# Three of eight k pairs by seven block products in each gate/up slice of a hybrid encoder block

## The chip, the cores and the metric

The kernel runs on one core of one Trainium2 chip. Its time is the device time of one execution in microseconds; the median of 3 runs of the kernel before is 1122.85 us (1122.55 to 1123.35).

## What is computed

One layer of an encoder block on 256 tokens of width 2048, in float32: RMSNorm, a projection, four mLSTM heads and four differential attention heads, an output projection, and then the part that matters here, SwiGLU with a hidden width of 5632:

```python
def swiglu(h, w_gate, w_up, w_down):
    return (jax.nn.silu(h @ w_gate) * (h @ w_up)) @ w_down

x = x + mixer(rms_norm(x, norm1_w), ...)
x = x + swiglu(rms_norm(x, norm2_w), w_gate, w_up, w_down)
```

## The kernel before

Every product with a weight matrix is made of three matmuls. An operand `a` is split in `a_hi` (a rounded to TensorE's fp32r) and `a_lo = a - a_hi`, and TensorE adds up `hi x w_lo + lo x w_hi + hi x w_hi`. The activations stand turned (`act_hi`, `act_lo`: 16 k tiles of 128 rows by 256 tokens); the weights are streamed.

The weights come in chunks of 128 x 1024 floats (512 KB). SyncE loads each into one of four places of `w_raw`; ScalarE writes `w_hi` from it, VectorE `w_lo`, both into one of four places (`SPLIT`), and TensorE uses them. Four semaphores carry this: `raw_landed`, `hi_done`, `lo_done` and `chunk_used`. ScalarE may write place n % 4 once chunk n - 4 is used; SyncE may load a raw place once VectorE has split what was there. Each engine has its own queue, in the order in which the program is written, and one use of a split chunk is called a step.

The input projection (96 chunks), the output projection (32) and the first of the eleven gate/up slices are written out. A slice is 512 columns of gate and the same 512 of up, for both token tiles, over 16 k tiles. Slices 2 to 11 run in a loop (`Fori`) on TensorE, ScalarE, VectorE and SyncE. The down projection follows (2 x 44 chunks).

In the looped slices two of the eight pairs of k tiles are handled by seven block products in place of eight. The two token tiles by the two k tiles of a pair are a 2 x 2 matrix of blocks, and the two k tiles by the gate's and the up's 512 columns are another. Seven products of sums of blocks suffice (`q1`, `q5`, `q7`, `q6` in the four `aux` banks, the other three right into `acc`), each of three matmuls: 21 in place of 24. The sums of activation blocks (E7, E5, E6, E3) are made once, in the first slice (`sum_hi`, `sum_lo`); those of weight blocks by VectorE in each slice, in place in `w_raw` (`weight_sums`: one of 1024 columns and two of 512 for a pair). A pair is four steps, of 3, 6, 6 and 6 matmuls; a single step has 12. So a slice has 12 single steps and 2 x 4, 20 steps and 186 matmuls.

Three steps behind the second pair ScalarE copies `q1` and VectorE combines the `aux` banks and adds them to the gate banks (`scaled`, with `pre_ready`) and, at the next slice's start, to the up banks (`hidden`). ScalarE then takes the SiLU of the gate (`gate`, `gate_act`), VectorE the product (`hid_ready`), TensorE turns it (`turn_hidden`), and both split it into `hid_hi` and `hid_lo`. TensorE waits at a slice's start for `gate_act`, behind the second step for `hid_ready`, and before the first pair for `hid_lo_done`.

Of the kernel before, what the change touches and what calls it, by code (L numbers as in the profile page):

```python
# [33 lines left out]
P = 128  # L34
# [16 lines left out]
RAW = 4  # L51
# [22 lines left out]
STEPS = 2 * 6 + 2 * 4  # L74
STEP0 = FF0 + FF_CHUNKS - STEPS
DOWN_STEP0 = STEP0 + FF_SLICES * STEPS
# [6 lines left out]
RELEASE = (-3, -2, -1, 0, 1, 2, 3, 4, 5, 8, 9, 10, 11, 12, 15, 16)  # L83
# [3 lines left out]
def step_raw(c):  # L87
    return c if c < 5 else c - 2 if c < 12 else c - 4

# [21 lines left out]
def hybrid_block_kernel(nc, x, x_turned, params, gate_bias, gate_w, weights, out):  # L111
    ctx = ExitStack()
    with ctx:
# [108 lines left out]
        seven = sb("seven", [3, NG], F32, ff)  # L222
        sum_hi = hid_hi[:, KF - 4:KF, :].rearrange("p k s -> p (k s)")
        sum_lo = hid_lo[:, KF - 4:KF, :].rearrange("p k s -> p (k s)")
        ff.close()
# [14 lines left out]
        evac_step = sem("evac_step")  # L240
        first_landed = sem("first_landed")
# [105 lines left out]
        def _(sp):  # L347
# [6 lines left out]
            for n in range(1, 8):  # L354
                if n < 5:
                    sp.dma_start(xt[:, xt_parts[n], :], x_turned[:, xt_parts[n], :]).then_inc(xt_landed[n], 16)
                if n >= RAW:
                    c = slice(NG * (n - RAW), NG * (n - RAW + 1))
                    sp.dma_start(res[:, :, c], x_t[:, :, c]).then_inc(x_landed[n - RAW], 16)
                    sp.wait_ge(lo_done, n - (RAW - 1))  # L360
                load(slice(n, n + 1), n % RAW)
            with sp.Fori(2, (FF0 + FF_CHUNKS) // RAW) as i:
                for k in range(RAW):
                    sp.wait_ge(lo_done, i * RAW + (k - (RAW - 1)))
                    load(bass.ds(i * RAW + k, 1), k)
# [4 lines left out]
            with sp.Fori(0, 2 * KF // RAW) as i:  # L370
                for k in range(RAW):
                    sp.wait_ge(lo_done, i * RAW + (DOWN_STEP0 + k - (RAW - 1)))
                    load(bass.ds(i * RAW + (DOWN0 + k), 1), k)
# [8 lines left out]
        def _(pool):  # L382
# [22 lines left out]
            pool.dma_start(w_if[:], gate_w).then_inc(wif_landed, 16)  # L405
            pool.dma_start(bias_if[:], gate_bias).then_inc(bias_landed, 16)
# [10 lines left out]
        def _(pe):  # L417
# [243 lines left out]
            def summed(e, j):  # L661
                cols = slice(2 * P * e + P * j, 2 * P * e + P * (j + 1))
                return sum_hi[:, cols], sum_lo[:, cols]

            q1, q5, q7, q6 = aux[2], aux[3], aux[0], aux[1]

            def pair(n, j):
                c, k = PAIR_STEP[j], PAIR_K[j]
                begin, end = j == 0, j == 1
                pe.wait_ge(lo_done, n + (c + 1))  # L670
                three(q1, *tile(k, 0), c % SPLIT, 0, begin, end).then_inc(chunk_used, 1)
                pe.wait_ge(lo_done, n + (c + 2))
                three(acc[0], *tile(k + 1, 0), (c + 1) % SPLIT, 0, False, end)
                three(acc[2], *summed(E3, j), (c + 1) % SPLIT, 1, begin, False).then_inc(chunk_used, 1)
                pe.wait_ge(lo_done, n + (c + 3))
                three(q5, *summed(E5, j), (c + 2) % SPLIT, 0, begin, end)
                three(q7, *summed(E7, j), (c + 2) % SPLIT, 1, begin, end).then_inc(chunk_used, 1)
                pe.wait_ge(lo_done, n + (c + 4))
                three(acc[1], *tile(k + 1, 1), (c + 3) % SPLIT, 0, False, end)
                three(q6, *summed(E6, j), (c + 3) % SPLIT, 1, begin, end).then_inc(chunk_used, 1)  # L680

            def ff_slice(i):
                n = i * STEPS + STEP0
                for c in range(STEPS):
                    if c == 0:
                        pe.wait_ge(gate_act, i * 2)
                    if c == PAIR_STEP[0]:
                        pe.wait_ge(hid_lo_done, i * 2)
                        pair(n, 0)
                    if c == PAIR_STEP[1]:  # L690
                        pair(n, 1)
                    if c in GATE_STEPS or c in UP_STEPS:
                        q = GATE_STEPS.index(c) if c in GATE_STEPS else UP_STEPS.index(c)
                        banks = acc[0:2] if c in GATE_STEPS else acc[2:4]
                        pe.wait_ge(lo_done, n + (c + 1))
                        for kk in range(2):
                            for t in range(TT):
                                begin = q == 0 and kk == 0 and (c in GATE_STEPS or t == 1)
                                end = q == 5 and kk == 1 and c in UP_STEPS
                                mm = three(banks[t], *tile(2 * q + kk, t), c % SPLIT, kk, begin, end)  # L700
# [812 lines left out]
```

## Time and profile before

| | us |
|---|---|
| median of 3 runs | 1122.85 |
| the profiled execution | 1125.04 |
| its span, first to last instruction | 1123.2 |
| TensorE busy with matmuls | 1113.3 |
| TensorE busy loading weights | 922.0 |
| VectorE busy | 734.6 |
| ScalarE busy | 576.8 |
| DMA, mean rate | 189 GB/s |

The span is what the rows can be laid against. Matmuls are pipelined: each is shown for some 0.39 us, while the next starts some 0.23 us after it, so TensorE's pace is read from start to start. Where VectorE's or ScalarE's instructions stand in one row with a count, the time is that of the whole run of them.

### The profile page before, as it was taken

What the parts mean: (1) busy time and instruction counts of PE and PEld (TensorE: products, weight loads), DVE (VectorE), ACT (ScalarE), POOL (GpSimd) and SP (SyncE); (2) the same over time, 40 slices, a digit from 0 to 9 for tenths busy, and PEclk for the clock granted to TensorE, in tenths of its full rate; (3) what the DMA queues carried; (4) which work ended last, traced back from release to release, by engine and by line L of the source; (5) the groups of instructions that cost most, each with busy time, mean ns of one, the idle gap of its engine ahead of it and who ended that gap; (6) DMA issues with size and microseconds to landing.
All of it is one profiled execution on the core that took longest, in us unless ns stands there. A gap on an engine that the chain in (4) does not pass through costs nothing.

```text
span 1123.2 us, 14985 instructions
## 1 busy us (share of the span) xinstructions
PE 1113.3 (99%) x5020; PEld 922.0 (82%) x5020; DVE 734.6 (65%) x876; ACT 576.8 (51%) x718; POOL 4.5 (0%) x20
## 2 busy tenths in 40 slices
PE   8999999999999999999999999999999999999998
PEld 6888887888888888888888888888888888888886
DVE  5566546764565566788787788788788644454443
ACT  7566466754545455446455455555555443343341
POOL 1000000000000000000000000000000000000000
PEclk8999999999999999999999999999999999999999
DMA  9555544564465646466566565565565756656554
GB/s 345 184 165 191 172 147 132 185 205 154 146 197 172 202 164 211 150 201 211 181 205 205 187 205 201 175 221 179 181 220 168 223 189 195 195 190 197 194 188 131
DMA packets 59796, 212.46 MB, mean 189 GB/s; under 512 B 6752, under 2 KB 6752, under 8 KB 59760
## 3 DMA queue, kind: packets, MB, share of 16 engines
q1 hardware_dynamic: 59552, 211.84, 57.1%
q8 instruction: 26, 0.43, 0.2%
q10 hardware_dynamic: 144, 0.05, 0.0%
q14 instruction: 10, 0.08, 0.0%
q0 software_dynamic: 64, 0.07, 0.0%
HBM read 209.83 MB, written 2.10 MB: 189 GB/s over the span
## 4 chain that ended last, share of the span: by engine, by line
PE 98%; DMA 1%; DVE 1%; ACT 0%; SPq 0%; issue 0%; ACTq 0%
PE acc L431 15%; PE acc L434 15%; PE acc L433 15%; PE acc L655 11%; PE acc L653 11%; PE acc L654 11%; PE aux L434 4%; PE aux L433 4%; PE aux L431 4%; PE aux L445 2%; PE aux L654 2%; PE aux L653 2%; PE aux L655 2%; DMA w_raw<-in_weights 1%; PE aux L495 0%; DVE res L1450 0%
## 5 line engine op out<-in xcount | busy, mean ns | idle before, releaser
L1060 DVE TENSOR_TENSOR w_lo<-w_raw,w_hi 128x1024 fp32r<-128x1024 f32 x231 | 280.8, 1223 | 241.1 <-ACT w_hi L750 119.6
L1393 DVE TENSOR_TENSOR w_lo<-w_raw,w_hi 128x1024 fp32r<-128x1024 f32 (+1 forms) x200 | 227.4, 1167 | 50.6 <-ACT w_hi L1008 23.6
L653 PE MATMUL acc<-w_lo,act_hi 128*128 128x512 f32 x520 | 203.2, 391 | 0.0
L655 PE MATMUL acc<-w_hi,act_hi 128*128 128x512 f32 x520 | 202.5, 389 | 0.0
L654 PE MATMUL acc<-w_hi,act_lo 128*128 128x512 f32 x520 | 202.3, 389 | 0.0
L750 ACT ACTIVATE w_hi<-w_raw 128x1024 fp32r<-128x1024 f32 x143 | 149.2, 1056 | 82.0 <-PE acc L434 73.9
L431 PE MATMUL acc<-w_lo,act_hi 128*128 128x512 f32 x448 | 179.1, 400 | 3.3 <-DVE w_lo L1060 3.3
L434 PE MATMUL acc<-w_hi,act_hi 128*128 128x512 f32 x448 | 175.7, 392 | 0.0
L433 PE MATMUL acc<-w_hi,act_lo 128*128 128x512 f32 x448 | 175.6, 392 | 0.0
L1011 ACT ACTIVATE w_hi<-w_raw 128x1024 fp32r<-128x1024 f32 x120 | 125.5, 1056 | 55.6 <-PE acc L655 32.2
L1032 ACT ACTIVATE w_hi<-w_raw 128x1024 fp32r<-128x1024 f32 x80 | 84.9, 1061 | 132.2 <-PE aux L434 132.2
L655 PEld LDWEIGHTS acc<-w_hi,act_hi 128*128 128x128 f32 x520 | 97.6, 188 | 20.4
L653 PEld LDWEIGHTS acc<-w_lo,act_hi 128*128 128x128 f32 x520 | 97.6, 188 | 20.0
L654 PEld LDWEIGHTS acc<-w_hi,act_lo 128*128 128x128 f32 x520 | 97.7, 188 | 19.9
L431 PEld LDWEIGHTS acc<-w_lo,act_hi 128*128 128x128 f32 x448 | 84.8, 189 | 22.4 <-issue 4.7
L434 PEld LDWEIGHTS acc<-w_hi,act_hi 128*128 128x128 f32 x448 | 84.8, 189 | 18.0
L433 PEld LDWEIGHTS acc<-w_hi,act_lo 128*128 128x128 f32 x448 | 84.9, 190 | 16.9
L431 PE MATMUL acc<-w_lo,hid_hi 128*128 128x512 f32 x176 | 68.6, 390 | 0.0
L431 PE MATMUL aux<-w_lo,hid_hi 128*128 128x512 f32 x176 | 68.5, 389 | 0.0
L434 PE MATMUL aux<-w_hi,hid_hi 128*128 128x512 f32 x176 | 68.5, 389 | 0.0
L434 PE MATMUL acc<-w_hi,hid_hi 128*128 128x512 f32 x176 | 68.5, 389 | 0.0
L433 PE MATMUL aux<-w_hi,hid_lo 128*128 128x512 f32 x176 | 68.5, 389 | 0.0
(250 smaller groups left out, 1274.4 us busy)
## 6 DMA issues: line engine op xcount, KB each, us to landing
w_raw<-in_weights SPq DMA_DIRECT2D x391, 512.0 KB, 4.2
res<-in_x SPq DMA_DIRECT2D x4, 512.0 KB, 10.8
out<-res SPq DMA_DIRECT2D x8, 256.0 KB, 3.8
xt<-in_x_turned SPq DMA_DIRECT2D x3, 512.0 KB, 9.4
xt<-in_x_turned SPq DMA_DIRECT2D x2, 256.0 KB, 4.3
w_raw<-in_weights SPq DMA_DIRECT2D x2, 256.0 KB, 3.8
w_if<-in_gate_w POOLq DMA_DIRECT2D x1, 64.0 KB, 6.7
par<-in_params ACTq DMA_DIRECT2D x1, 47.0 KB, 3.6
```

The lines of the kernel that those rows point to most:

```text
L431: pe.matmul(bank[:], hi[:, k, tok], w_lo[:, slot, cols], start=first and kk == 0, stop=False)
L433: pe.matmul(bank[:], lo[:, k, tok], w_hi[:, slot, cols], start=False, stop=False)
L434: mm = pe.matmul(bank[:], hi[:, k, tok], w_hi[:, slot, cols], start=False, stop=last and kk == len(kts) - 1)
L445: mm = pe.transpose(banks[t][:, P * b:P * (b + 1)], src[:, t, P * b:P * (b + 1)], ident[:])
L653: pe.matmul(bank[:], hi, w_lo[:, slot, cols], start=start, stop=False)
L654: pe.matmul(bank[:], lo, w_hi[:, slot, cols], start=False, stop=False)
L655: return pe.matmul(bank[:], hi, w_hi[:, slot, cols], start=False, stop=stop)
L750: act.activation(w_hi[:, slot, :], w_raw[:, slot, :], ACT.Copy).then_inc(hi_done, 1)
L1011: act.activation(dst, w_raw[:, step_raw(c) % RAW, :], ACT.Copy).then_inc(hi_done, 1)
L1032: act.activation(w_hi[:, c, :], w_raw[:, c, :], ACT.Copy).then_inc(hi_done, 1)
L1060: dve.tensor_tensor(w_lo[:, slot, :], w_raw[:, slot, :], w_hi[:, slot, :].bitcast(F32), ALU.subtract).then_inc(lo_done, 1)
L1393: dve.tensor_tensor(w_lo[:, c % SPLIT, cols], w_raw[:, slot, cols], w_hi[:, c % SPLIT, cols].bitcast(F32), ALU.subtract).then_inc(lo_done, 1)
```

## The change

A third pair of k tiles goes by seven products (k tiles 10 and 11, beside 12, 13 and 14, 15), in slices 2 to 11. The order of steps in such a slice is now a string, `ggggPguPuPuuu` (g a gate step, u an up step, P a pair of four steps); before it was five gate steps, a pair, a gate step, two up steps, a pair, four up steps. A slice has 10 single steps and 3 x 4, 22 steps. `plan()` lists every step of the program, and all engines' loops are written out from that list. `w_raw` has eight places in place of four, and a load waits for the last use of what stands in its place (`LAST_USE`). The tile `seven` is gone; its contents stand in `stage` and `gated`. The third pair's activation sums (`third_hi`, `third_lo`) are made in the first slice. The evacuation begins two steps behind the last pair (`EVAC_AT` 20, `PAIR_END` 18), with four of VectorE's operations in front of the next split in place of three. TensorE waits at a slice's start for `pre_ready` in place of `gate_act`. The loads of `gate_w` and `gate_bias` go from GpSimd's queue to ScalarE's, behind its work for chunk 1. The code also holds a way to handle pairs of the down projection, which `DOWN_PAIRS = ((), ())` leaves unused.

```diff
-RAW = 4
+RAW = 8
-GATE_STEPS = (0, 1, 2, 3, 4, 9)
-UP_STEPS = (10, 11, 16, 17, 18, 19)
-PAIR_STEP = (5, 12)
-PAIR_RAW = (5, 10)
-PAIR_K = (12, 14)
+SLICE_ORDER = "ggggPguPuPuuu"
+HALF = SLICE_ORDER.count("g")
+N_PAIRS = SLICE_ORDER.count("P")
+PAIR_K = [12, 14, 10][:N_PAIRS]
+EVAC_AT = 20
...
 SyncE
-            with sp.Fori(1, FF_SLICES) as i:
-                for j in range(FF_CHUNKS):
-                    sp.wait_ge(lo_done, i * STEPS + (STEP0 + RELEASE[j]))
-                    load(bass.ds(i * FF_CHUNKS + (FF0 + j), 1), j % RAW)
+            for n in range(RAW, CHUNKS):
+                sp.wait_ge(lo_done, LAST_USE[n - RAW] + 1)
+                load(slice(n, n + 1), n % RAW)
 GpSimd, ScalarE
-            pool.dma_start(w_if[:], gate_w).then_inc(wif_landed, 16)
-            pool.dma_start(bias_if[:], gate_bias).then_inc(bias_landed, 16)
+                if n == 1:
+                    act.dma_start(w_if[:], gate_w).then_inc(wif_landed, 16)
+                    act.dma_start(bias_if[:], gate_bias).then_inc(bias_landed, 16)
...
 TensorE
+            def ff_pair(i, n, j):
+                q1, q5, q7, q6 = aux[2], aux[3], aux[0], aux[1]
+                k, begin, end = PAIR_K[j], j == 0, j == N_PAIRS - 1
+                pe.wait_ge(lo_done, n + 1)
+                three(q1, *tile(k, 0), n % SPLIT, 0, begin, end).then_inc(chunk_used, 1)
+                pe.wait_ge(lo_done, n + 2)
+                three(acc[0], *tile(k + 1, 0), (n + 1) % SPLIT, 0, False, end)
+                three(acc[2], *summed(E3, j), (n + 1) % SPLIT, 1, begin, False).then_inc(chunk_used, 1)
+                pe.wait_ge(lo_done, n + 3)
+                if begin:
+                    pe.wait_ge(hid_lo_done, 2 * i)
+                three(q5, *summed(E5, j), (n + 2) % SPLIT, 0, begin, end)
+                three(q7, *summed(E7, j), (n + 2) % SPLIT, 1, begin, end).then_inc(chunk_used, 1)
+                pe.wait_ge(lo_done, n + 4)
+                three(acc[1], *tile(k + 1, 1), (n + 3) % SPLIT, 0, False, end)
+                three(q6, *summed(E6, j), (n + 3) % SPLIT, 1, begin, end).then_inc(chunk_used, 1)
-                        pe.wait_ge(gate_act, i * 2)
+                        pe.wait_ge(gate_act, 2)
+                        if i >= 2:
+                            pe.wait_ge(pre_ready, 2 * (i - 1))
-            with pe.Fori(1, FF_SLICES) as i:
+            for i in range(1, FF_SLICES):
                 ff_slice(i)
...
 ScalarE
-                    if c == PAIR_STEP[1] + 6:
-                        act.wait_ge(chunk_used, i * STEPS + (STEP0 + PAIR_STEP[1] + 4))
-                        act.activation(seven[:, 0, :], aux[2][:], ACT.Copy).then_inc(q1_copied, 1)
+                    if c == EVAC_AT:
+                        act.wait_ge(chunk_used, SLICE_START[i] + PAIR_END + 1)
+                        act.wait_ge(hid_ready, 2 * i)
+                        act.activation(gated[:, 1, :], aux[2][:], ACT.Copy).then_inc(q1_copied, 1)
 VectorE
+                    if c == LAG and N_PAIRS == 3:
+                        dve.wait_ge(x1_squared, 4)
+                        dve.wait_ge(turn_lo, 10)
+                        dve.tensor_tensor(gated[:, 0, :], ..., ALU.add).then_inc(third_full, 1)
+                        dve.wait_ge(third_full, 1)
+                        block_sums([[third[:, h, t, :] for t in range(TT)] for h in range(2)],
+                                   [third_e[:, m, :] for m in range(4)], third_step, 0).then_inc(third_step, 1)
...
+                    if c == EVAC_AT:
+                        dve.wait_ge(q1_copied, i)
+                        dve.wait_ge(hid_turned, 2 * i)
+                        dve.tensor_tensor(stage[:, 1, :], aux[1][:], gated[:, 1, :], ALU.subtract).then_inc(evac_step, 1)
+                        dve.tensor_tensor(scaled[:, 0, :], acc[0][:], gated[:, 1, :], ALU.add).then_inc(pre_ready, 1)
+                        dve.wait_ge(evac_step, 6 * i - 1)
+                        dve.wait_ge(pre_ready, 2 * i - 1)
+                        dve.tensor_tensor(gated[:, 1, :], aux[0][:], stage[:, 1, :], ALU.subtract).then_inc(evac_step, 1)
+                        dve.wait_ge(evac_step, 6 * i)
+                        dve.tensor_tensor(scaled[:, 1, :], acc[1][:], gated[:, 1, :], ALU.add).then_inc(pre_ready, 1)
```

VectorE's order in the kernel before, from the second (last) pair of a slice on: the half split, the three sums of weight blocks (`w_raw<-w_raw`) and the splits between them.

```order
L1393 TENSOR_TENSOR w_lo<-w_raw,w_hi 128x512
L1402 REGISTER_ALU
L1403 TENSOR_TENSOR w_raw<-w_raw 128x1024
L1385 REGISTER_ALU
L1393 TENSOR_TENSOR w_lo<-w_raw,w_hi 128x1024
L1407 TENSOR_TENSOR w_raw<-w_raw 128x512
L1409 TENSOR_TENSOR w_raw<-w_raw 128x512
L1385 REGISTER_ALU
L1393 TENSOR_TENSOR w_lo<-w_raw,w_hi 128x1024
L1385 REGISTER_ALU
L1393 TENSOR_TENSOR w_lo<-w_raw,w_hi 128x1024
L1385 REGISTER_ALU
```

The same engine in the changed kernel, from the last sum of a slice's second pair to the end of its third and the first operation of the evacuation.

```order
L1160 TENSOR_TENSOR w_raw<-w_raw 128x512
L1143 TENSOR_TENSOR w_lo<-w_raw,w_hi 128x1024 x3
L1143 TENSOR_TENSOR w_lo<-w_raw,w_hi 128x512
L1154 TENSOR_TENSOR w_raw<-w_raw 128x1024
L1143 TENSOR_TENSOR w_lo<-w_raw,w_hi 128x1024
L1158 TENSOR_TENSOR w_raw<-w_raw 128x512
L1160 TENSOR_TENSOR w_raw<-w_raw 128x512
L1143 TENSOR_TENSOR w_lo<-w_raw,w_hi 128x1024 x4
L1511 TENSOR_TENSOR stage<-aux,gated 128x512
```

Behind the second pair's last two splits stands one single step's split, and then the third pair begins; the register instructions between the operations are gone.

VectorE's order around the evacuation, in the kernel before: two splits, three operations on the product banks, a split, and then the rest.

```order
L1393 TENSOR_TENSOR w_lo<-w_raw,w_hi 128x1024
L1385 REGISTER_ALU
L1393 TENSOR_TENSOR w_lo<-w_raw,w_hi 128x1024
L1424 TENSOR_TENSOR seven<-aux,seven 128x512
L1425 TENSOR_TENSOR scaled<-acc,seven 128x512
L1426 REGISTER_ALU
L1428 TENSOR_TENSOR seven<-aux,seven 128x512
L1385 REGISTER_ALU
L1393 TENSOR_TENSOR w_lo<-w_raw,w_hi 128x1024
L1430 TENSOR_TENSOR seven<-aux,seven 128x512
L1432 TENSOR_TENSOR scaled<-acc,seven 128x512
```

And in the changed kernel.

```order
L1143 TENSOR_TENSOR w_lo<-w_raw,w_hi 128x1024 x4
L1511 TENSOR_TENSOR stage<-aux,gated 128x512
L1513 TENSOR_TENSOR scaled<-acc,gated 128x512
L1516 TENSOR_TENSOR gated<-aux,stage 128x512
L1519 TENSOR_TENSOR scaled<-acc,gated 128x512
L1143 TENSOR_TENSOR w_lo<-w_raw,w_hi 128x1024
L1521 TENSOR_TENSOR stage<-aux,stage 128x512
L1523 TENSOR_TENSOR stage<-stage,aux 128x512
```

The second addition into `scaled` has moved in front of the split.

## Rows read from the trace of the kernel before

**Rows 1.** The page, sections 1 and 2 (tenths of each fortieth).

```profile
PE 1113.3 (99%) x5020; PEld 922.0 (82%) x5020; DVE 734.6 (65%) x876; ACT 576.8 (51%) x718; POOL 4.5 (0%) x20
...
PEclk8999999999999999999999999999999999999999
```

**Rows 2.** The page, section 4, the chain that ended last.

```profile
PE 98%; DMA 1%; DVE 1%; ACT 0%; SPq 0%; issue 0%; ACTq 0%
```

**Rows 3.** Chain in order of time (start us, us, what): transposes.

```profile
346.23 0.87 PE aux L445 x8
368.91 0.87 PE aux L445 x8
...
539.37 0.87 PE aux L445 x8
582.45 0.87 PE aux L445 x8
```

**Rows 4.** First and looped slice: us, busy (x) of PE, PEld, DVE, ACT, POOL; clock, DMA, GB/s.

```profile
410.31:453.39 43.08, 43.08 (x197) 35.76 (x196) 27.68 (x33) 21.78 (x23) 0.00 (x0) 1.00 0.61 193
582.63:625.71 43.08, 43.08 (x197) 35.77 (x196) 35.12 (x38) 22.85 (x25) 0.00 (x0) 1.00 0.59 195
```

**Rows 5.** Timeline of PE (start us, us): the second pair begins.

```profile
604.26 0.39 PE L653 MATMUL aux<-w_lo,act_hi 128*128 128x512 f32 x1
```

**Rows 6.** Timeline of ACT: last part of pair two, copy of q1.

```profile
604.46 1.06 ACT L1008 ACTIVATE w_hi<-w_raw 128x1024 fp32r<-128x1024 f32 x1 [1.66 <-PE acc L655]
...
609.22 0.60 ACT L1020 ACTIVATE seven<-aux 128x512 f32<-128x512 f32 x1
```

**Rows 7.** Timeline of DVE: pairs one and two, evacuation.

```profile
585.03 0.68 DVE L1393 TENSOR_TENSOR w_lo<-w_raw,w_hi 128x512 fp32r<-128x512 f32 x1
585.85 1.23 DVE L1403 TENSOR_TENSOR w_raw<-w_raw 128x1024 f32<-128x1024 f32 x1
...
599.78 1.23 DVE L1403 TENSOR_TENSOR w_raw<-w_raw 128x1024 f32<-128x1024 f32 x1 [0.99 <-DMA w_raw<-in_weights]
600.93 1.22 DVE L1393 TENSOR_TENSOR w_lo<-w_raw,w_hi 128x1024 fp32r<-128x1024 f32 x1
602.19 0.69 DVE L1407 TENSOR_TENSOR w_raw<-w_raw 128x512 f32<-128x512 f32 x1
602.92 0.69 DVE L1409 TENSOR_TENSOR w_raw<-w_raw 128x512 f32<-128x512 f32 x1
603.53 1.22 DVE L1393 TENSOR_TENSOR w_lo<-w_raw,w_hi 128x1024 fp32r<-128x1024 f32 x1
605.55 3.50 DVE L1393 TENSOR_TENSOR w_lo<-w_raw,w_hi 128x1024 fp32r<-128x1024 f32 x3 [0.81 <-ACT w_hi L1008]
...
610.41 0.68 DVE L1424 TENSOR_TENSOR seven<-aux,seven 128x512 f32<-128x512 f32 x1
611.01 0.68 DVE L1425 TENSOR_TENSOR scaled<-acc,seven 128x512 f32<-128x512 f32 x1
611.79 0.69 DVE L1428 TENSOR_TENSOR seven<-aux,seven 128x512 f32<-128x512 f32 x1
612.40 1.22 DVE L1393 TENSOR_TENSOR w_lo<-w_raw,w_hi 128x1024 fp32r<-128x1024 f32 x1
```

**Rows 8.** Timeline of all engines at the start.

```profile
0.74 0.41 ACTq L758 DMA_DIRECT2D par<-in_params  x1
...
4.02 0.73 POOL L405 DMA_DIRECT2D w_if<-in_gate_w  x1
...
12.11 0.76 PE L431 MATMUL acc<-w_lo,act_hi 128*128 128x512 f32 x1 [2.75 <-DVE w_lo L1060]
...
13.58 1.22 DVE L1060 TENSOR_TENSOR w_lo<-w_raw,w_hi 128x1024 fp32r<-128x1024 f32 x1
...
17.37 0.63 PE L431 MATMUL acc<-w_lo,act_hi 128*128 128x512 f32 x1
```

**Rows 9.** The same columns as group 4, for the stretch behind PE's first idle time.

```profile
12.10:18.00 5.90, 5.89 (x14) 4.64 (x15) 5.87 (x12) 5.61 (x12) 0.00 (x0) 0.50 1.03 401
```

More of the change, by code:

```diff
@@ L20 @@
 import math
+from collections import namedtuple
 from contextlib import ExitStack
@@ new lines, with sum_place, plan, add_pair @@
+HALF = SLICE_ORDER.count("g")
+N_PAIRS = SLICE_ORDER.count("P")
+PAIR_K = [12, 14, 10][:N_PAIRS]
+DOWN_PAIRS = ((), ())
+SUM_BLOCKS = (slice(4, 6), slice(6, 8), slice(3, 9, 5), slice(1, 3))
+SUM_AT = (5, 9, 13, 17)
+E7, E5, E6, E3 = range(4)
+def sum_place(k):
+    m = k // 4
+    g = next(g for g in range(4) if m in range(*SUM_BLOCKS[g].indices(KF // 4)))
+    return g, list(range(*SUM_BLOCKS[g].indices(KF // 4))).index(m)
+def plan():
+    steps = [Step("one", n, n, 0, 0) for n in range(FF0 + FF_CHUNKS)]
+    load, pair, starts = FF0 + FF_CHUNKS, 0, []
+    def add_pair(index):
+        nonlocal load, pair
+        for part in range(4):
+            steps.append(Step("pair", index, load, part, pair))
+        load, pair = load + 2, pair + 1
+    for i in range(1, FF_SLICES):
+        starts.append(len(steps))
+        count = {"g": 0, "u": 0, "P": 0}
+        for kind in SLICE_ORDER:
+            if kind == "P":
+                add_pair(count["P"])
+            else:
+                steps.append(Step(kind, count[kind], load, 0, 0))
+                load += 1
+            count[kind] += 1
+    for p in range(2):
+        starts.append(len(steps))
+        k = 0
+        while k < KF:
+            if k in DOWN_PAIRS[p]:
+                add_pair(k)
+                k += 2
+            else:
+                steps.append(Step("one", k, load, 0, 0))
+                load, k = load + 1, k + 1
+    return steps, starts
@@ new lines @@
+PLAN, STARTS = plan()
+SLICE_START = [FF0] + STARTS[:FF_SLICES - 1]
+DOWN_START = STARTS[FF_SLICES - 1:]
+STEPS = SLICE_START[2] - SLICE_START[1]
+LAST_USE = {st.load + (st.part == 3): n for n, st in enumerate(PLAN) if st.kind != "pair" or st.part >= 2}
+PAIR_END = max(c for c in range(STEPS) if PLAN[SLICE_START[1] + c].kind == "pair")
+EVAC_AT = 20
+DOWN_PAIR_END = [max([n for n in range(DOWN_START[p], len(PLAN)) if PLAN[n].kind == "pair"
+                      and (p or n < DOWN_START[1])], default=0) for p in range(2)]
@@ new lines, in ff_slice @@
+            def ff_slice(i):
+                for n in range(SLICE_START[i], SLICE_START[i] + STEPS):
+                    st = PLAN[n]
+                    if n == SLICE_START[i]:
+                        pe.wait_ge(gate_act, 2)
+                        if i >= 2:
+                            pe.wait_ge(pre_ready, 2 * (i - 1))
+                    if st.kind == "pair" and st.part == 0:
+                        ff_pair(i, n, st.index)
+                    if st.kind in ("g", "u"):
+                        banks = acc[0:2] if st.kind == "g" else acc[2:4]
+                        pe.wait_ge(lo_done, n + 1)
@@ L728, in _ @@
                         pe.wait_ge(hid_lo_done, 2 * FF_SLICES)
-                    chunk(DOWN_STEP0 + p * KF + k, k % SPLIT, banks, (k,), 2, hid_hi, hid_lo,
-                          k == 0, k == KF - 1, p == 1 and k == KF - 1)
+                    if st.kind == "pair" and st.part == 0:
+                        down_pair(p, n, k)
+                    if st.kind == "one":
+                        chunk(n, n % SPLIT, banks, (k,), 2, hid_hi, hid_lo,
+                              k == 0, k == KF - 1, p == 1 and k == KF - 1)
                     if p == 0 and k == LAG:
```

416 lines of the change are left out of this document (232 added, 184 removed).

## The prediction, made before the changed kernel had run

> **What bounds the kernel now.** I read the busy shares first, then the chain of waits, then the pace of TensorE in code written out and in the loop, and last the order in time of VectorE and ScalarE in one slice. TensorE (PE) is busy for 1113.3 of 1123.2 us, in every fortieth of the span but the first and the last, and its granted clock is full after the start [rows 1]. A busy PE is not yet a PE at its pace, so the chain must say the same: 98% of it is PE [rows 2]. The pace itself: between the transposes at 346.23 and 368.91 (the output projection, written out) lie 8 transposes of together 0.87 us and 8 chunks of 12 matmuls, (22.68 - 0.87) / 96 = 0.2272 us each. Between 539.37 and 582.45 (one pass of the loop) lie 43.08 us, 8 transposes and 186 matmuls: 42.21 / 186 = 0.2269 us [rows 3]. The two agree, so nothing but PE's own stream sets the time of a gate/up slice, and the loop's branch costs nothing. In that slice VectorE (DVE) works 35.12 of 43.08 us and ScalarE (ACT) 22.85 [rows 4]: both wait for PE, through the ring of four split chunks. What PE no longer has to do is gained in full, for as long as DVE delivers.
>
> **What the change removes from PE.** A slice had 12 single steps of 12 matmuls and two pairs of 21. It gets 10 singles and three pairs: 120 + 63 = 183. Ten slices lose 30 matmuls, and 30 x 0.2269 = 6.81 us, all on the path. The first slice, the projections and the down stage keep their counts.
>
> **What it adds on DVE.** Number the steps of a new slice 0 to 21: four gate steps, pair 4-7, gate 8, up 9, pair 10-13, up 14, pair 15-18, up 19-21. Per slice come one more full subtraction (1.22), one half (0.69), and three sums (1.23, 0.69, 0.69): 4.5 us by the rows [rows 7], so 39.6 busy of a slice of 43.08 - 0.68 = 42.4. It fits, but the average decides nothing; a pair takes 4.77 us of PE and nearly 7 of DVE, and the third pair follows the second after a single step. So I follow that place.
>
> DVE is even with the ring before pair two: step 7 starts 1.29 after PE ends step 3 (0.20 for the release, 604.26 to 604.46; 1.06 for ACT's half of the split; 0.03 to DVE, 605.55) [rows 5 to 7]. Steps 7, 8, 9 follow at 1.14 each (three in 3.50: (3.50 - 1.22) / 2), then pair two's opening: 0.82 (585.03 to 585.85), 1.15, 1.26, 0.73, 0.61 from 599.78 to 603.53 [rows 7]. Step 12 starts at 9.28 and leaves DVE free at 10.42 after the end of step 3; the ring admits step 13 only at 10.21 + 1.29 = 11.50. A second of slack: nothing of pair two's load is carried over.
>
> From the end of step 9 on (time 0) the chain is 1.29 to the start of step 13, 1.14 to 14, 1.14 to 15, 0.82 to the sum behind the half, 1.15 to step 16, 1.26 and 0.73 to its two sums, 0.61 to step 17, and 1.22 for it: 9.36 us. PE wants step 17 after pair two, a single and 9 matmuls, 4.77 + 2.72 + 2.04 = 9.53. Slack 0.17, where the kernel before has 0.89 at its tightest, the last part of its pair two: begun at 605.55 and ready at 606.77, wanted 15 matmuls (3.40) after 604.26. Step 18 waits for the last sum, ACT's 1.06 and DVE: ready at 10.56, wanted at 10.89. Step 19: 11.70 against 12.25. The handoffs may be shorter, since the register instructions that stood ahead of each are gone: the half, if it passes on like the sums do (0.69 + 0.04), gives 0.09 back.
>
> How long ahead of its first matmul a step must be ready no row shows well. If one matmul's time (0.23, while weights load) is wanted, the 0.17 misses by 0.06. I take 0.05 us lost per slice, 0.5 in all; the ends are 0 and 0.15 a slice.
>
> **The evacuation.** It stood three steps behind its pair and stands two behind now, with four operations ahead of the next split where there were three. Let T be PE's end of step 18. ACT's copy of q1 begins at T + 0.20, takes 0.60 [rows 6], and DVE at T + 0.83 does 0.60, 0.78, 0.78 (the third's result is waited for, like that at 611.01 to 611.79) and 0.60 [rows 7]; step 21 starts at T + 3.56 and is ready at T + 4.78. PE wants it at T + 5.44: hidden, 0.66 to spare. ACT's next split waits behind the copy, ready at about T + 2, which is early enough. Behind step 21 the last two operations and step 22 end at T + 7.3, wanted at 8.16. The old wait of PE for the second SiLU at a slice's start becomes one for DVE's addition, earlier by the SiLU and its handoff; it was hidden and stays so.
>
> **The other edits.** The ring of eight raw chunks takes away ACT's and DVE's waits for DMA within a slice, which PE never saw: 0, hidden by the split ring; its loads run ahead at the start only behind the loads that are needed sooner, in the same queue. The third pair's activation sums come once, in the first slice: at most six operations of at most 0.69, 4.1 us, where DVE idles 43.08 - 27.68 = 15.4 us [rows 4]. Writing the loops out: 0 by the two paces above. The two small loads move from GpSimd's queue at 4.02 to ACT's behind its work for chunk 1 [rows 8]: two issues of 0.41 each (the one ACT issue in the trace) ahead of chunk 2's split. DVE's part of that split ends at 13.58 + 1.22 = 14.80 and PE takes chunk 2 at 17.37, late because it runs chunk 1 at the half clock (0.50 from 12.10 to 18.00 [rows 9]). With 0.82 added it still comes 1.7 us early, so 0.
>
> On the loops the Trainium skill ("Runtime: NRT & Kernel Launch", Instruction fetch mechanics) says that a taken branch whose target is not in the fetched window stalls for a fetch, and that straight code streams. By it each pass of the loop could have cost something that now comes back; the paces of 0.2269 and 0.2272 show none, so the sum has none.
>
> **Sum.** 6.8 - 0.5 = 6.3 us. The profiled execution would go from a span of 1123.2 to 1116.9 and, with the 1.84 around it, from 1125.04 to 1118.7. The median of the runs, 1122.85, lies 2.19 below the profiled one, so the forecast is 1116.5.
>
> **Rivals.**
> *DVE is late at step 17.* If none of its operations overlapped the one before, four links of the chain (two of 1.14, 1.15, 0.61) grow by 0.08: 9.68, late by 0.15, with weight loading up to 0.4 a slice. Loss 1.5 to 4 us: 1117.5 to 1120. For it: the slack of 0.17 is sum of ten handoffs. Against: the three operations in 3.50 us do overlap.
> The rule behind this rival is the Trainium skill's ("VectorE: DVE Perf Modes", The DRAIN you can't avoid): the next operation doesn't start until the pipe is empty. By it the sum would be nearer 5; the trace's 1.14 from start to start against 1.22 of duration disagrees.
>
> *The start shifts.* PE idles 2.75 us for chunk 1 and then runs at half clock [rows 8]. With 64 KB less beside chunk 1's load it may land sooner and the clock may not fall: 14 matmuls at 0.43 instead of 0.23 are 2.8 us, with the idle 3.3. The other way is as possible, and as large. 1113.5 or 1119.5.
>
> *Slower.* The evacuation decides: PE needs step 21, DVE has four PSUM operations in front of it, and ACT holds the next splits behind the copy. It costs from the point where step 21 comes more than 0.66 later than T + 4.78, and makes the kernel slower from 1.34 (0.66 + 0.68); a handoff of 0.5 at each of the three semaphores of that chain beside the lateness of rival one would do it. At 1.0 us of stall per slice, 10 - 6.8 = 3.2 us more: 1126. For it: such chains of small waits are easily undercounted. Against: the same operations take 0.60 to 0.78 apiece in the trace.
>
> *It doesn't do what it says:* the written-out PE order has 183 matmuls a slice, so this is out.
>
> **Chances.** Forecast (1115.8 to 1117.4) 0.63; DVE late at step 17, 0.20; the start, 0.09; the evacuation, 0.08, half of that over 1125.1 and half between 1120.6 and there. A measurement of this kernel tells 0.2%, 2.2 us. The first three are faster even at their upper ends: 0.92. I move 0.03 of it to no change and 0.01 to slower for what I have not seen: faster 0.88, same 0.04 + 0.03 = 0.07, slower 0.04 + 0.01 = 0.05. The range of 8 in 10 runs from 1115.3 to 1119.3: it holds the forecast, most of the first rival and a milder shift of the start.
>
> **What the profile will show.** Right: transposes of neighbouring slices 42.4 to 42.5 us apart where they were 43.08, 30 matmuls fewer, PE without idle time, DVE busy for about 39.5 us of a slice, its split of step 17 without idle time before it. Wrong: a slice of over 42.7 us, PE idle ahead of the third part of pair three (step 17) or of step 21 with DVE as the releaser, an end of the half clock other than at 18 us, or idle time of PE that no engine released, which would be code fetched late.

## The result and the profile after

| | before | after |
|---|---|---|
| median of 4 runs, us | 1122.7 | 1115.05 (1114.8 to 1115.3) |
| the profiled execution | 1125.04 | 1114.8 |
| its span | 1123.2 | 1113.0 |

The change makes the kernel 7.65 us faster: a ratio of 0.9931, with a 95% interval of 0.9914 to 0.9948. The forecast was 1116.5, in a range from 1115.3 to 1119.3; the kernel is 0.25 us below the range's lower end.

The page of the changed kernel: TensorE has its 30 matmuls less, its clock is full from the start, and VectorE works 778 us where it worked 734.6 [rows 1].

```profile
PE 1105.3 (99%) x4990; PEld 914.8 (82%) x4990; DVE 778.0 (70%) x932; ACT 590.6 (53%) x739; POOL 3.3 (0%) x18
...
PEclk9999999999999999999999999999999999999999
```

Its chain in order of time (start us, us, what). The first row stands for the start, the next two for written-out code as before, then two neighbouring slices, and last VectorE's work behind the last matmuls.

```profile
46.73 0.87 PE aux L494 x8
...
343.75 0.87 PE aux L494 x8
366.43 0.87 PE aux L494 x8
...
535.58 0.87 PE aux L494 x8
578.01 0.87 PE aux L494 x8
...
1107.74 2.73 DVE res L1583 x4
```

The slices are 42.43 us apart where they were 43.08 [rows 3]; over the nine from 450.75 to 832.51 it is 42.42. The output projection has kept its 22.68. So the slices give 10 x 0.66 = 6.6 us. The windows of that slice (columns as in [rows 4]):

```profile
535.58:578.00 42.42, 42.42 (x193) 35.15 (x192) 39.23 (x43) 24.19 (x27) 0.00 (x0) 1.00 0.61 200
```

VectorE is busy 39.23 of 42.42 us (39.6 was forecast, from 35.12 in [rows 4]) and PE waits for nothing. The answer to [rows 5 to 7] is the third pair. TensorE, VectorE and ScalarE in the timeline; 552.23 is the release after the end of step 9, which is therefore at 552.03:

```profile
561.50 0.39 PE L702 MATMUL aux<-w_lo,third_hi 128*128 128x512 f32 x1
```

```profile
553.33 2.96 DVE L1143 TENSOR_TENSOR w_lo<-w_raw,w_hi 128x1024 fp32r<-128x1024 f32 x3 [1.11 <-ACT w_hi L845]
556.32 1.22 DVE L1154 TENSOR_TENSOR w_raw<-w_raw 128x1024 f32<-128x1024 f32 x1
557.46 1.22 DVE L1143 TENSOR_TENSOR w_lo<-w_raw,w_hi 128x1024 fp32r<-128x1024 f32 x1
558.72 0.69 DVE L1158 TENSOR_TENSOR w_raw<-w_raw 128x512 f32<-128x512 f32 x1
559.44 0.69 DVE L1160 TENSOR_TENSOR w_raw<-w_raw 128x512 f32<-128x512 f32 x1
560.05 4.71 DVE L1143 TENSOR_TENSOR w_lo<-w_raw,w_hi 128x1024 fp32r<-128x1024 f32 x4
565.07 0.69 DVE L1511 TENSOR_TENSOR stage<-aux,gated 128x512 f32<-128x512 f32 x1 [0.31 <-ACT gated L1100]
...
566.46 0.69 DVE L1516 TENSOR_TENSOR gated<-aux,stage 128x512 f32<-128x512 f32 x1
567.19 0.69 DVE L1519 TENSOR_TENSOR scaled<-acc,gated 128x512 f32<-128x512 f32 x1
567.80 1.22 DVE L1143 TENSOR_TENSOR w_lo<-w_raw,w_hi 128x1024 fp32r<-128x1024 f32 x1
```

```profile
552.23 2.67 ACT L845 ACTIVATE w_hi<-w_raw 128x1024 fp32r<-128x1024 f32 x3 [1.66 <-PE acc L704]
...
564.44 0.60 ACT L1100 ACTIVATE gated<-aux 128x512 f32<-128x512 f32 x1 [1.31 <-PE aux L704]
```

Steps 13, 14 and the half of 15 are the row at 553.33; then come the sum, step 16, its two sums, and at 560.05 step 17, which is ready at 561.27 (560.05 + 1.22). From 552.03 that is 9.24 us, where the prediction counted 9.36: the half passes on to the sum after 0.71 (1.14 + 1.14 + 0.71 = 2.99) and not after 0.82. PE takes step 17 at 561.50, one matmul's 0.23 behind its predecessor at 561.27, without a gap; that is 9.47 from 552.03, where 9.53 was counted. So the slack is 0.23 us, where it was to be 0.17. The evacuation is at its reckoned place too: the copy ends at 565.04, VectorE starts at 565.07 and step 21 at 567.80, 2.73 later (2.76 was counted).

What was not forecast lies behind the last matmuls, in what is called the tail from here on. From the start of VectorE's last additions to the end of the span it is 1123.2 - 1116.77 = 6.43 us before and 1113.0 - 1107.74 = 5.26 after. Before, the same two rows of the chain and the windows around the output's writes are:

```profile
49.22 0.87 PE aux L445 x8
...
1116.77 2.73 DVE res L1450 x4
```

```profile
1119.00:1120.00 1.00, 0.00 (x0) 0.00 (x0) 0.49 (x1) 0.00 (x0) 0.00 (x0) 1.00 1.12 359
1120.00:1121.00 1.00, 0.00 (x0) 0.00 (x0) 0.00 (x0) 0.00 (x0) 0.00 (x0) 1.00 1.11 215
1121.00:1122.00 1.00, 0.00 (x0) 0.00 (x0) 0.00 (x0) 0.00 (x0) 0.00 (x0) 1.00 0.88 219
```

And after, the same stretch:

```profile
1110.00:1111.00 1.00, 0.00 (x0) 0.00 (x0) 0.47 (x1) 0.00 (x0) 0.00 (x0) 1.00 1.02 379
1111.00:1112.00 1.00, 0.00 (x0) 0.00 (x0) 0.00 (x0) 0.00 (x0) 0.00 (x0) 1.00 1.01 385
1112.00:1113.00 1.00, 0.00 (x0) 0.00 (x0) 0.00 (x0) 0.00 (x0) 0.00 (x0) 0.65 0.07 23
```

The last columns are the DMA engines' share and GB/s. The output leaves at 359 and then 215 and 219 GB/s before, at 379 and 385 after, with the DMA engines busy all the time in both. The four transfers by the view of DMA issues, before and after, microseconds to landing at the end:

```profile
out<-res SPq DMA_DIRECT2D x4, 256.0 KB, 3.1
```

```profile
out<-res SPq DMA_DIRECT2D x4, 256.0 KB, 2.2
```

### The profile page after: what moved, and what is told of

Its sections match the earlier page's. It is cut to its first block, busy times and chain, and to the rows that moved or that the text cites. A ratio compares the mean times of both kernels' runs of the same rounds, so it can differ in the third digit from the quotient of the medians.

```text
span 1113.0 us, 12848 instructions
## 1 busy us (share of the span) xinstructions
PE 1105.3 (99%) x4990; PEld 914.8 (82%) x4990; DVE 778.0 (70%) x932; ACT 590.6 (53%) x739; POOL 3.3 (0%) x18
## 4 chain that ended last, share of the span: by engine, by line
PE 97%; DMA 1%; DVE 1%; ACT 1%; issue 0%; ACTq 0%
PE acc L480 15%; PE acc L483 15%; PE acc L482 15%; PE acc L704 10%; PE acc L702 10%; PE acc L703 10%; PE aux L482 4%; PE aux L483 4%; PE aux L480 4%; PE aux L703 2%; PE aux L702 2%; PE aux L704 2%; PE aux L494 2%; DMA w_raw<-in_weights 1%; DMA par<-in_params 0%; PE aux L544 0%
## 5 line engine op out<-in xcount | busy, mean ns | idle before, releaser
L1143 DVE TENSOR_TENSOR w_lo<-w_raw,w_hi 128x1024 fp32r<-128x1024 f32 (+1 forms) x451 | 524.8, 1186 | 264.2 <-ACT w_hi L845 262.6
L845 ACT ACTIVATE w_hi<-w_raw 128x1024 fp32r<-128x1024 f32 (+1 forms) x451 | 456.0, 1028 | 353.5 <-PE aux L483 137.3
L480 PE MATMUL acc<-w_lo,act_hi 128*128 128x512 f32 x448 | 178.2, 398 | 2.3 <-DVE w_lo L1143 2.3
L702 PE MATMUL acc<-w_lo,act_hi 128*128 128x512 f32 x460 | 179.9, 391 | 0.0
L704 PE MATMUL acc<-w_hi,act_hi 128*128 128x512 f32 x460 | 179.1, 389 | 0.0
L703 PE MATMUL acc<-w_hi,act_lo 128*128 128x512 f32 x460 | 179.0, 389 | 0.0
L483 PE MATMUL acc<-w_hi,act_hi 128*128 128x512 f32 x448 | 174.7, 390 | 0.0
L482 PE MATMUL acc<-w_hi,act_lo 128*128 128x512 f32 x448 | 174.5, 389 | 0.0
L480 PEld LDWEIGHTS acc<-w_lo,act_hi 128*128 128x128 f32 x448 | 84.1, 188 | 21.7 <-issue 4.2
L703 PEld LDWEIGHTS acc<-w_hi,act_lo 128*128 128x128 f32 x460 | 86.4, 188 | 17.7
L702 PEld LDWEIGHTS acc<-w_lo,act_hi 128*128 128x128 f32 x460 | 86.4, 188 | 17.6
L482 PEld LDWEIGHTS acc<-w_hi,act_lo 128*128 128x128 f32 x448 | 84.2, 188 | 16.6
L482 PE MATMUL acc<-w_hi,hid_lo 128*128 128x512 f32 x176 | 68.5, 389 | 0.0
L480 PE MATMUL acc<-w_lo,y_hi 128*128 128x512 f32 x128 | 50.2, 392 | 0.0
L483 PE MATMUL acc<-w_hi,y_hi 128*128 128x512 f32 x128 | 49.9, 390 | 0.0
```

The source lines that it names most:

```text
L480: pe.matmul(bank[:], hi[:, k, tok], w_lo[:, slot, cols], start=first and kk == 0, stop=False)
L482: pe.matmul(bank[:], lo[:, k, tok], w_hi[:, slot, cols], start=False, stop=False)
L483: mm = pe.matmul(bank[:], hi[:, k, tok], w_hi[:, slot, cols], start=False, stop=last and kk == len(kts) - 1)
L702: pe.matmul(bank[:], hi, w_lo[:, slot, cols], start=start, stop=False)
L703: pe.matmul(bank[:], lo, w_hi[:, slot, cols], start=False, stop=False)
L704: return pe.matmul(bank[:], hi, w_hi[:, slot, cols], start=False, stop=stop)
```

## The experiments

### What the other edits bring: two pairs, and the ring

The changed kernel with two pairs a slice, then the same with a ring of four:

```diff
-SLICE_ORDER = "ggggPguPuPuuu"
+SLICE_ORDER = "gggggPguuPuuuu"
-EVAC_AT = 20
+EVAC_AT = 18
 and in the second kernel also
-RAW = 8
+RAW = 4
-            for n in range(RAW, CHUNKS):
+            for n in range(8, CHUNKS):
```

> The changed kernel with two pairs per slice again (gggggPguuPuuuu, evacuation three steps behind), all else as in the change: ring of eight, loops written out, small loads on ScalarE, the smaller scratch. Theory A (the third pair gives 10 x 0.66 = 6.6 us, and about 1.0 us comes from the other edits, in the tail's output DMA or at the start): 1121.7 us, slices of 43.08 us. Rival B (the other edits give nothing and the rest lies in the pair): 1122.7 us.

> As the run with two pairs, but with four raw chunks in the ring in place of eight. If the ring of eight brings the rest of about 1 us (its loads end sooner, or start sooner), this is at 1122.7; if the moved small loads, the smaller scratch or the written-out loops bring it, 1121.7 like the two-pair kernel.

Measured: 1121.2 us (0.9987 of before, 0.9977 to 0.9997) and 1121.38 us (0.9991, 0.9981 to 1.0). The chain of the first:

```profile
46.61 0.87 PE aux L494 x8
...
536.72 0.87 PE aux L494 x8
579.80 0.87 PE aux L494 x8
...
1114.11 2.73 DVE res L1583 x4
```

Its slices take 43.08 us. So theory A holds, with its second size too small: the third pair is worth 6.15 us by the medians and 6.49 from the first transposes to the last additions, and about 1.3 us, where theory A has 1.0, come from other edits. The ring is not among them: 0.2 us is within the spread of the runs.

### The small loads and the scratch

The change also sets the scratch for dynamic DMAs to 2048, which its description above does not name. The kernel before with one of these edits each, and a third time with both:

```diff
-            pool.dma_start(w_if[:], gate_w).then_inc(wif_landed, 16)
-            pool.dma_start(bias_if[:], gate_bias).then_inc(bias_landed, 16)
+                if n == 1:
+                    act.dma_start(w_if[:], gate_w).then_inc(wif_landed, 16)
+                    act.dma_start(bias_if[:], gate_bias).then_inc(bias_landed, 16)
 the other
-    nc = bacc.Bacc("TRN2", target_bir_lowering=False, num_devices=1)
+    nc = bacc.Bacc("TRN2", target_bir_lowering=False, num_devices=1, dynamic_dma_scratch_size=2048)
```

> The kernel before, with only the loads of gate_w and gate_bias moved from GpSimd's queue to ScalarE's behind its work for chunk 1. Theory A1 (64 KB less beside chunk 1's load, and no software queue beside it: chunk 1 lands some 0.8 us sooner, TensorE's first idle time is 1.1 to 2.0 and not 2.75 us, and no stretch at the half clock follows): 1121.7 us, and less where the kernel before has that stretch. Rival (the start is what it is, the rest comes from elsewhere): 1122.7 us.

> The kernel before with only the scratch for dynamic DMAs set to 2048. Theory A2 (it is the addresses or the descriptors of the transfers that changed: the last four output transfers take some 1.2 us less together): 1121.7 us, output rate near 380 GB/s at the end in place of 230. Rival: 1122.7 us and the output as before.

> The kernel before with the small loads on ScalarE's queue and the smaller scratch together, so that nothing uses the software queue: 2.9 us for the last output packets if rival E's pair of edits does it, else 3.9 us.

Measured: 1122.62 us (ratio 1.0, 0.999 to 1.0009), 1122.57 us (1.0, 0.999 to 1.001), and 1123.41 us in one run for both. Neither edit alone does anything that these runs can tell, and both together don't shorten the tail. The chain of the kernel with the moved loads, and its window from 12 to 18 us:

```profile
46.61 0.87 PE aux L443 x8
...
1114.12 2.73 DVE res L1451 x4
```

```profile
12.00:18.00 6.00, 6.00 (x27) 4.70 (x26) 5.92 (x12) 4.98 (x10) 0.00 (x0) 1.00 1.04 395
```

The first transposes come at 46.61 and not at 49.22, at a full clock where [rows 9] have 0.50. But so they do without the moved loads: at 46.92 with the smaller scratch alone, and between 46.46 and 47.27 in the eight other kernels below that keep the start of before. The half clock behind PE's first idle time comes and goes from execution to execution: four of the nineteen profiled ones have it, the one of before (1125.04, 2.3 us over the median) with a mean granted clock of 0.50 from 14 to 17 us, and in shorter stretches one kernel with the start of before (five slices written out first, 0.83 from 14 to 17 us) and two with the moved loads (both edits, 0.70; two pairs and SyncE's loops, 0.85). So it goes with neither start, and the runs show no effect of the change on it. All three tails are the long ones, 6.48, 6.48 and 6.49 us.

### Whose loop it is

SyncE's loops written out in the kernel before, and the complement (two pairs, ring of four, only SyncE looped):

```diff
-            with sp.Fori(1, FF_SLICES) as i:
-                for j in range(FF_CHUNKS):
-                    sp.wait_ge(lo_done, i * STEPS + (STEP0 + RELEASE[j]))
-                    load(bass.ds(i * FF_CHUNKS + (FF0 + j), 1), j % RAW)
...
+            for n in range(8, CHUNKS):
+                sp.wait_ge(lo_done, waits[n])
+                load(slice(n, n + 1), n % RAW)
```

> The kernel before with only SyncE's loops written out, with the same waits, places and order of loads. The kernels with all loops written out end 1.2 us sooner behind their last matmul: their last 576 output packets take 2.89 us in place of 3.89. Theory S (the descriptors or registers of SyncE's looped loads are what disturbs the output's writes): tail as in the change, 1121.4 us. Rival C (not SyncE, but the other engines' code or where the program and its tensors lie): tail of 3.9 us, 1122.5 us.

> The complement: two pairs, ring of four, all engines written out but SyncE, which has the kernel before's loops. Theory S: tail of 3.9 us, 1122.5 us. Rival C: tail of 2.9 us, 1121.4 us.

Measured: 1122.89 us (1.0001, 0.9991 to 1.001) with a tail of 6.54 us, and 1121.22 us (0.9987, 0.9977 to 0.9996) with a tail of 5.25. Theory S falls.

Then the compute engines' loops, in the kernel before: all three, TensorE's alone, the other two alone.

```diff
-            with pe.Fori(1, FF_SLICES) as i:
+            for i in range(1, FF_SLICES):
 and for ScalarE and VectorE
-            with act.Fori(1, FF_SLICES) as i:
+            for i in range(1, FF_SLICES):
...
```

> The kernel before with the loops of TensorE, ScalarE and VectorE written out, SyncE's looped, nothing else changed (ring of four, the tile seven, small loads on GpSimd). Theory D (the written-out loops of the compute engines are what shortens the output's writes): the last 576 output packets take 2.9 us, 1121.4 us. Rival E (another edit of the change does it: the tiles' new places without seven, or the small loads and the scratch together): 3.9 us, 1122.6 us.

> The kernel before with only TensorE's loop written out. If its 2 x 1,700 further instructions matter (the size of the program and where it and the output lie): output packets in 2.9 us, else 3.9 us.

> The kernel before with only ScalarE's and VectorE's loops written out. Output packets in 2.9 us if one of these two engines' loops matters, 3.9 us if TensorE's does or none.

Measured: 1121.29 us (0.9987, 0.9978 to 0.9997), tail 5.34; one run of 1121.28, tail 5.36; one run of 1122.95, tail 6.50. It is TensorE's loop, and writing it out brings nothing but the shorter tail: the slices stay 43.05 to 43.09 us apart in all three.

Last, how much of it, and where. Five slices written out behind a loop of five, five written out ahead of a loop of five, one written out behind a loop of nine, and the loop kept beside an unread input:

```diff
-            with pe.Fori(1, FF_SLICES) as i:
+            with pe.Fori(1, 6) as i:
+                ff_slice(i)
+            for i in range(6, FF_SLICES):
                 ff_slice(i)
 the second
+            for i in range(1, 6):
+                ff_slice(i)
+            with pe.Fori(6, FF_SLICES) as i:
 the third
+            with pe.Fori(1, FF_SLICES - 1) as i:
+                ff_slice(i)
+            ff_slice(FF_SLICES - 1)
 the fourth
+        "pad": np.zeros((13, P, 32), np.float32),
```

> The kernel before with five of TensorE's ten looped slices kept in the loop and five written out behind it. If the size of the code decides (a place that shifts with it), the output packets may take either 2.9 or 3.9 us; if it is the loop's presence, 3.9 us; if it is that TensorE comes to the down stage out of written-out code, 2.9 us.

> The kernel before with TensorE's first five looped slices written out and the last five in the loop: the code is as long as with the loop first. If the amount of code decides: last output packets in 2.9 us. If it is what TensorE runs right before the down stage: 3.9 us.

> The kernel before with only the last gate/up slice of TensorE written out behind the loop. If the amount of code decides, and a slice's worth is too little: 3.9 us. If it is what TensorE runs right before the down stage: 2.9 us.

> The kernel before with one more input of 13 x 128 x 32 floats (208 KB, about what TensorE's written-out loop adds in code) that nothing reads. Theory F (the output's writes depend on where the output lies in memory, which more bytes ahead of it shift): 2.9 us. Rival (the place is not it, or this input doesn't shift it): 3.9 us.

Measured, each in one run: 1121.38, 1121.88, 1122.7 and 1122.29 us, with tails of 5.27, 5.28, 6.47 and 6.49 us. The order of loop and written-out code makes no difference, the amount of written-out code does; each of the four is one run, but their tails fall clearly on one side or the other. On the page, queue q8 of the code fetches, which grows with TensorE's code alone (packets, MB, share), has this for one slice written out and for five:

```profile
q8 instruction: 27, 0.44, 0.2%
```

```profile
q8 instruction: 33, 0.54, 0.2%
```

The kernel before has 26 such packets, the changed one 39. Over all nineteen profiled executions the tail falls in two groups and nothing between: 6.43 to 6.54 us in the eight with 26 or 27 packets, 5.23 to 5.36 in the eleven with 33 or 39. In the windows of the tail of the kernel before and of the changed one all packets are the output's own (576 on q1), and in the last 12 us of none of the nineteen is there a packet of code, so it isn't a fetch of code beside the writes that disturbs them. What the length of the code changes there stays open. The place of the output in memory would be a guess: the unread input, which was meant to shift it, did nothing, but no run shows where the output lies, so the guess is neither shown nor ruled out.

### How exact the chain on VectorE is

The third pair right behind the second, with the same work in all:

```diff
-SLICE_ORDER = "ggggPguPuPuuu"
+SLICE_ORDER = "ggggPguuPPuuu"
```

> The changed kernel with the third pair right behind the second (ggggPguuPPuuu), same counts of matmuls and of all other work. By the chain of handoffs of the prediction, counted from the end of step 10: step 14 starts at 1.29, the half of 15 at 2.43, its sum at 3.14, step 16 at 4.28, the sums at 5.54 and 6.26, step 17 at 6.87 and is ready at 8.09, where TensorE wants it at 6.81: late by 1.3 and a little for step 16, 1.4 us a slice, 1115.05 + 14 = 1129 us, with TensorE's idle time in front of step 17 (aux matmuls) released by VectorE. Rival (VectorE's slack is larger than the chain says, or the ring gives way elsewhere): under 1122 us. Rival (each VectorE operation waits for the one before to end, no overlap): 1131 us or more.

Measured: 1130.16 us (1.0068 of before, 1.0051 to 1.0085), 15.1 us over the changed kernel. Neighbouring transposes:

```profile
538.38 0.87 PE aux L494 x8
...
582.33 0.87 PE aux L494 x8
```

43.95 us, 1.53 more than 42.42. VectorE's first sum of pair three, its steps 16 and 17, and TensorE's first matmul behind step 10 and those that wait for steps 16 and 17:

```profile
560.71 1.22 DVE L1154 TENSOR_TENSOR w_raw<-w_raw 128x1024 f32<-128x1024 f32 x1
561.85 1.22 DVE L1143 TENSOR_TENSOR w_lo<-w_raw,w_hi 128x1024 fp32r<-128x1024 f32 x1
...
564.44 2.43 DVE L1143 TENSOR_TENSOR w_lo<-w_raw,w_hi 128x1024 fp32r<-128x1024 f32 x2
```

```profile
557.49 0.39 PE L702 MATMUL aux<-w_lo,act_hi 128*128 128x512 f32 x1
...
563.12 0.50 PE L702 MATMUL acc<-w_lo,act_hi 128*128 128x512 f32 x1
563.46 0.40 PE L703 MATMUL acc<-w_hi,act_lo 128*128 128x512 f32 x1
...
565.71 0.50 PE L702 MATMUL aux<-w_lo,third_hi 128*128 128x512 f32 x1 [0.94 <-DVE w_lo L1143]
566.05 0.39 PE L703 MATMUL aux<-w_hi,third_lo 128*128 128x512 f32 x1
```

The weight load of the first of these matmuls of step 17 (PEld) starts at the same moment as the matmul; elsewhere in the stream it starts some 0.22 us ahead:

```profile
565.71 0.19 PEld L702 LDWEIGHTS aux<-w_lo,third_hi 128*128 128x128 f32 x1 [1.36 <-DVE w_lo L1143]
```

Step 17 is ready at 564.44 + 1.22 = 565.66, and TensorE begins it 0.05 later. The place and the kind of wait are as the chain said, and the split is ready 8.11 us behind the end of step 10 (at 557.55) against 8.09. What the chain left out is the price of being late: behind such a wait the second matmul starts 0.34 after the first in place of 0.23. The first matmul behind step 10 starts at 557.49; step 17 stands 30 matmuls (6.81 us) behind it and would have begun at 564.30. It begins 1.41 later, and the 0.11 behind it makes 1.52, of the 1.53 that a slice is longer. Step 16's own lateness is no further term, since TensorE would only have waited longer for step 17. The total of 1130.16 alone would not tell the chain from the rival without overlap (1131 or more); the trace does: steps ready at 8.11 and starts 1.14 apart (560.71 to 561.85) are the chain with overlap. The slack is not larger either.

The evacuation a step earlier:

```diff
-EVAC_AT = 20
+EVAC_AT = 19
```

> The changed kernel with the evacuation one step earlier, right behind the split of step 19 (EVAC_AT 19). With T the end of step 18, the copy ends at T + 0.80, VectorE's four operations take 2.73 and the split of step 20 is ready at T + 4.78, where TensorE wants it at T + 2.72: 2.1 us of stall a slice, 1115.05 + 21 = 1136 us. It tests the point from which the evacuation decides. Rival (its operations overlap with TensorE's queue or the split goes first): 1115 to 1120 us.

Measured: 1140.75 us (1.016, 1.0143 to 1.0177), 25.7 over the changed kernel where 21 was expected. TensorE's wait (total, times, longest) is where it was expected, at a step of gate or up behind pair three. Two neighbouring slices, then a stretch behind the wait in the first of them, and last the greater part of the last slice show what came on top (columns as in [rows 4], the granted clock third from the end):

```profile
PE acc L702 <- DVE w_lo L1143: 19.5, 10, 1.9
```

```profile
541.55:587.88 46.33, 44.39 (x194) 36.22 (x192) 39.50 (x44) 24.17 (x27) 0.00 (x0) 0.96 0.55 182
587.88:632.53 44.65, 42.70 (x194) 35.09 (x192) 39.38 (x44) 24.17 (x27) 0.00 (x0) 1.00 0.56 188
576.90:580.00 3.10, 3.10 (x9) 2.39 (x8) 2.82 (x3) 0.64 (x1) 0.00 (x0) 0.50 0.79 263
855.84:898.00 42.16, 40.22 (x175) 32.85 (x173) 35.41 (x40) 23.54 (x26) 0.00 (x0) 0.96 0.55 187
```

A slice takes 44.65 us, 2.23 more than the changed kernel's: the wait, and again the 0.11 behind it. In three of the ten, the ones that start at 450.57, 541.55 and 855.84, the clock then falls: granted 0.50, its lower level of 1.2 GHz, while some eight starts of matmuls are 0.43 apart. The first two of them take 46.33 us, 1.68 more. For this execution that makes 10 x 2.23 + 3 x 1.68 = 27.3 us, and its span is 1140.2 - 1113.0 = 27.2 longer than the changed kernel's. Its time, 1142.04, is the longest of the four; the other three (1140.57 to 1140.79) would fit two such stretches, but no trace of them shows it.

### Pairs where VectorE has room

The two experiments say that a pair costs nothing as long as VectorE's chain keeps up. In the down projection it has more room, and the code for it was there:

```diff
-DOWN_PAIRS = ((), ())
+DOWN_PAIRS = ((18, 22, 26, 30, 34), (6, 10, 14, 18, 22, 26, 30, 34))
```

> The changed kernel with pairs in the down projection too: k = 18, 22, 26, 30, 34 in the first pass, 6, 10, ..., 34 in the second, 13 pairs. The same price per pair: 13 x 3 x 0.2269 = 8.85 us less on TensorE, 1106.2 us. VectorE has 1.22 of every 2.72 us to do there, a pair costs it 7 us of 10.2 with the two single steps behind it, so it should keep up; rival: the sums of hidden blocks come late for k = 18 or the product banks are freed late between the passes, each 1 to 3 us once: 1107 to 1110 us.

Measured: 1106.58 us (1105.74 to 1108.18 in 4 runs), 0.9861 of the kernel before (0.9845 to 0.9878), and the fastest here: 8.5 us under the changed kernel, 8.8 from the first transposes to the span's end. The down stage and VectorE's last additions:

```profile
880.00:1100.00 220.00, 220.00 (x977) 182.27 (x975) 180.04 (x194) 112.47 (x115) 0.00 (x0) 1.00 0.56 182
```

```profile
1098.56 1.37 DVE L1583 TENSOR_TENSOR res<-res,acc 128x512 f32<-128x512 f32 x2 [6.46 <-PE acc L483]
```

VectorE works 180 of 220 us (102.93 of the 226 from 890 to 1116 before) and PE waits for nothing there. The reckoned 8.85 us (13 x 3 x 0.2269) is the whole of it.

## Why the prediction was right and where it was wrong

*TensorE's stream sets the time; 30 matmuls are 6.8 us.* Right. The slices gave 6.6 us, and the run with two pairs, all else as in the change, shows that they come from the third pair.

*0.05 us lost per slice at step 17.* The chain was right to 0.12 us (9.24 for 9.36), the loss was nearly nothing. Step 17 was ready 0.23 us ahead of its first matmul, and that was early enough: its twelve matmuls took 2.74 us (561.50 to 564.24) for the reckoned 2.72. A step that comes late loses the 0.11 that the run with adjacent pairs shows. The term of 0.5 us measured about 0.2, 42.42 for the reckoned 42.40 a slice, ten times.

*Writing the loops out: 0.* This is the step that failed. Its argument, equal paces in looped and written-out code, was right for what it looked at, and every slice of 43.08 us with the loops written out confirms it. But it was applied to the whole program, and the effect lay in the one stretch where TensorE's pace says nothing, behind its last matmul. It is worth 6.43 - 5.26 = 1.17 us, and TensorE's loop alone brings it (5.36 with only that loop written out). Why more TensorE code shortens the output's writes stays open. With the stall at its measured 0.2 and this term, the sum is 1122.7 - 6.8 + 0.2 - 1.2 = 1114.9, against the measured 1115.05. The forecast's base, 1122.85, was 0.15 above the median of four runs as well.

The Trainium skill ("Runtime: NRT & Kernel Launch", Instruction fetch mechanics) says that a branch stalls when its target is not in the fetched window, and that straight code streams. No run here shows that stall. The branch cost nothing in any of ten passes, and while the loop runs (453 to 884 us) the queue q8 fetches 2 packets of code, where the written-out code fetches 15 (453 to 875). What TensorE's longer code did, it did in the tail, where no code is fetched, so that the kernel got faster with straight code is no support for the rule.

*The evacuation is hidden.* Right: step 21 was ready at 567.80 + 1.22 = 569.02, 0.66 us before TensorE wanted it (564.24 + 5.44). That this is the predicted 0.66 to the hundredth is luck: the prediction's own terms, 0.83 and 2.76, add up to 3.59 and not to its 3.56, and the four operations took 2.73. The rival that put its turning point there was sound; one step earlier it costs 2.23 us a slice for the reckoned 2.1, and 1.7 us more whenever the clock falls.

*The ring of eight, the small loads, the third pair's sums: 0.* Right for all. The first two were tried; for the sums the trace shows it, since from the transposes ahead of the first slice to those behind it there are 38.98 us in both kernels (414.25 to 453.23 and 411.77 to 450.75).

*DVE late at step 17.* Its condition, that VectorE's operations do not overlap, didn't come true: 1.14 from start to start again. The section of the Trainium skill behind it ("VectorE: DVE Perf Modes", The DRAIN you can't avoid) has, beside the rule that the prediction tells, the exception that an operation that is not held starts earlier. These traces show the exception: in the changed kernel and in the one with adjacent pairs an operation of 1.22 us starts 1.14 after one of 1.22.

*The start shifts.* It did in the profiled executions, by 2.5 us (first transposes at 49.22 and 46.73), and this accounts for 1125.04 against 1122.7. As a term it was nothing, because the forecast was made from the median of runs that lie 1.7 to 2.5 us under that execution. With the small loads moved it came too (0.70 in the run of both edits), so they had no part in it that shows.

## What to carry to other kernels

Where one engine's stream sets the time, price a change by that stream, and prove that the helpers keep up by adding up the handoffs at the tightest place, from the last point at which the ring holds them back; busy shares (92% of a slice on VectorE here, with no wait of TensorE for it) don't tell. The same sum says which order of steps is free and which costs 15 us. Before an edit is put at zero, ask for each stretch of the span what shows that: the head and the tail have other bounds than the body, and a range that ends 1.2 us below the forecast has no room for an unpriced 1.2. Longer TensorE code is no recipe: what makes the tail short here is not known.

## What was not expected of the hardware

- The last 1 MB of output goes out in the same four transfers, but one takes 3.1 us to land (median) in the kernel before and 2.2 in the changed one, and the late part of the writes runs at 215 to 219 GB/s against 379 to 385. It switches between one and five slices' worth of written-out TensorE code; the tails of all eight kernels on the one side, and of all eleven on the other, agree within 0.13 us.
- Behind a wait of TensorE of 1.9 us in each slice the granted clock fell to the lower level (1.2 GHz) in three of ten slices, for some eight matmuls at 0.43 us; at 541.55 it fell only 1.5 us after TensorE had gone on (from 575.05 to 576.54). Behind a wait of 0.94 us in each of ten it did not in the profiled execution.
- Behind a wait for VectorE's split the weight load starts together with its matmul, and the next matmul follows after 0.34 us in place of 0.23. TensorE resumes 0.05 us after the end of the split that it waits for.
